# Experts 1 to 7 of a routed SwiGLU alternate the other way round: most tokens first, then fewest

## The chip, the cores and the metric

The kernel runs on one core of one Trainium2 chip. The metric is the device time of one execution in microseconds (us). The kernel before takes 1568.33 us, the median of three runs (1568.23 to 1573.31 us).

## What is computed

The reference is a two-layer streaming encoder on 256 tokens of width 1024, all in float32. Layer 0 has a pooling and state-space mixer and a dense feed-forward; layer 1 has a Mamba-2 mixer and then a routed feed-forward with eight experts, of which each token uses two. The change touches the order of the experts in that last part alone:

```python
def _moe_swiglu(h, w_router, b_router, w_gate, w_up, w_down):
    ...
    top_logit, top_idx = lax.top_k(logits, TOP_K)          # TOP_K = 2
    top_w = jax.nn.softmax(top_logit, axis=-1)
    ...
    for e in range(N_EXPERTS):                              # 8
        y_e = _swiglu(tok, w_gate[e], w_up[e], w_down[e])   # 1024 -> 3584 -> 1024
        out = out + gates[:, e:e + 1] * y_e
```

The sum over the experts can be taken in any order. Each expert has 3 x 1024 x 3584 float32 weights, 44.0 MB, and all eight are used.

## The kernel before

The routed part runs from about 714 us to the end. The weights of one expert come from HBM in 42 pieces of 1 MiB (`ITEM = 42`), in the fixed order `ORDER`: four steps t over the hidden columns, each with a gate product (`g`), an up product (`u`) and, one step later, the down product (`d`). Steps 0 to 2 have four pieces of each kind, step 3 has two of each. SyncE issues all these loads (line 462, in `load_expert`), expert after expert in one unbroken stream. They go round through 20 places in SBUF (`PIECES = 20`: 14 halves of `ring` and 6 areas of `arena`), so piece n may only be issued when TensorE has used piece n - 20; `first_pass_ready` waits for that on the semaphore `tile_used`. TensorE waits for each piece to land before it uses it (lines 1925 and 1961 are the matmuls of `hidden` and `output` in `expert`).

The experts are worked on in eight turns. Turn 0 is always expert 0, since its weights are loaded before the routing is known. The routing (lines 1225 to 1267) counts each expert's tokens. `make_turns` (lines 1284 to 1312, VectorE) then gives experts 1 to 7 their turns: `rank` is the number of experts with fewer tokens (0 to 6, ties broken by the number of the expert), and lines 1297 to 1300 turn the rank into a place from 1 to 7. A table of counts, flags and expert numbers by turn (`turn_i`) is released by `turns_ready`; SyncE takes the expert's number of each turn from it before it loads that expert's pieces, and TensorE, VectorE and ScalarE take the count, from which they choose one of three forms of the same program: (blocks, tokens a block) = (1, 64) up to 64 tokens, (3, 32) for 65 to 96, (2, 64) above. The form sets how long TensorE takes for a piece. The three forms use the same pieces in the same order.

Between two turns TensorE gathers the tokens of the next expert (`gather`, line 1417), scatters the outputs of the expert before the present one (`scatter`, line 1897) and turns hidden columns (line 1942). In the last turn the gather is replaced by the gate rows (line 1466). After the last turn come a last scatter, the norm and the store.

The lines of the rule before:

```python
c.inc(ts(place[:, 1:NE], rank, -2.0, 2.0 * n, ALU.mult, ALU.add), step)   # n = 7: 14 - 2 rank
c.then(ts(rank, rank, 2.0, 1.0, ALU.mult, ALU.add), step)                 # 2 rank + 1
...
c.then(tt(place[:, 1:NE], place[:, 1:NE], rank, ALU.min), step)
```

Of the kernel before, what the change touches and what calls it, by code (L numbers as in the profile page):

```python
# [13 lines left out]
ALU = mybir.AluOpType  # L14
# [19 lines left out]
NE = 8  # L34
# [92 lines left out]
def hybrid_trunk(nc, a, out):  # L127
    with ExitStack() as ctx:
# [774 lines left out]
        def _(dve):  # L903
            c = Counted(dve)
            v = nc.vector
            tt, ts, stt = v.tensor_tensor, v.tensor_scalar, v.scalar_tensor_tensor
            step = "dve_step"
# [192 lines left out]
            for t in range(6):  # L1100
                for j in range(2 if t == 5 else 4):
                    n = 4 * t + j
# [181 lines left out]
            def make_turns():  # L1284

                n = NE - 1
                own = totals[:, 1:NE].unsqueeze(2).broadcast_to([P, n, n])
                other = totals[:, 1:NE].unsqueeze(1).broadcast_to([P, n, n])
                less = order_tmp[:, 0:n * n].rearrange("p (e f) -> p e f", e=n)
                same = order_tmp[:, 64:64 + n * n].rearrange("p (e f) -> p e f", e=n)  # L1290
                rank, place = rt[:, 1, 0, 1:NE], rt[:, 1, 1]
                c.inc(tt(less, other, own, ALU.is_lt), step)
                c.then(tt(same, other, own, ALU.is_equal), step)
                c.then(tt(same, same, earlier[:, 1:NE, 1:NE], ALU.mult), step)
                c.then(tt(less, less, same, ALU.add), step)
                c.then(v.tensor_reduce(rank, less, AX.X, ALU.add), step)
                c.inc(ts(place[:, 1:NE], rank, -2.0, 2.0 * n, ALU.mult, ALU.add), step)
                c.then(ts(rank, rank, 2.0, 1.0, ALU.mult, ALU.add), step)
                c.inc(v.memset(place[:, 0:1], 0.0), step)
                c.then(tt(place[:, 1:NE], place[:, 1:NE], rank, ALU.min), step)  # L1300
                c.then(tt(perm, place.unsqueeze(1).broadcast_to([P, NE, NE]),
                          slot_iota[:, 0:NE].unsqueeze(2).broadcast_to([P, NE, NE]), ALU.is_equal), step)
                moved = order_tmp[:, 0:6 * NE * NE].rearrange("p (k c e) -> p k c e", k=NE, c=6)
                table = slots_of[:, 0].rearrange("p e b i -> p (b i) e").unsqueeze(1).broadcast_to([P, NE, 6, NE])
                c.then(tt(moved, table, perm.unsqueeze(2).broadcast_to([P, NE, 6, NE]), ALU.mult), step)
                c.then(v.tensor_reduce(slots_by_turn, moved, AX.X, ALU.add), step)
                rows_ = order_tmp[0:1, 0:3 * NE * NE].rearrange("p (j k e) -> p j k e", j=3, k=NE)
                for j, row in enumerate((cnt_f[:, 0:NE], cnt_f[:, 17:17 + NE], slot_iota[0:1, 0:NE])):
                    c.inc(tt(rows_[:, j], perm[0:1], row.unsqueeze(1).broadcast_to([1, NE, NE]), ALU.mult), step)
                dve.wait_ge(s[step], c.n[step])  # L1310
                c.then(v.tensor_reduce(turn_f.rearrange("p (j k) -> p j k", j=3), rows_, AX.X, ALU.add), step)
                c.inc(v.tensor_copy(turn_i[:, :], turn_f[:, :]), "turns_ready")
# [71 lines left out]
            take_tokens(0, MOE0)  # L1384
            take_gates(0, gates_of[0], 0)
            make_turns()
            dve.wait_ge(s["turns_ready"], 1)
            for e in range(NE):
# [689 lines left out]
```

How the kernel before makes its waits and increments, by code:

```python
            def then(self, ins, name):  # L332
                self.inc(ins, name)
                self.eng.wait_ge(s[name], self.n[name])
# [12 lines left out]
        def past(eng, name, n):  # L347
            eng.wait_ge(s[name], n + 1)
# [25 lines left out]
        def first_counts(eng, name):  # L375
            for primed in PRIMED[name]:
                eng.sem_inc(s[primed], 1)
            eng.wait_ge(s["cnt_ready"], 1)
# [25 lines left out]
        @block.sync  # L405
# [58 lines left out]
            def first_pass_ready(n):  # L464
                at = PLACES[n % PIECES]
                if n < PIECES and at < PIECES0 - 2:
                    sp.wait_ge(s["tile_used"], LAST_OF[at // 2] + 1)
                elif n < PIECES and at < PIECES0:
                    sp.wait_ge(s["y1_mm"], NB * NG)
                    sp.wait_ge(s["cb_mm"], NB * NG)
                elif n < PIECES and ARENA_PIECES[at - PIECES0] == 0:
                    sp.wait_ge(s["z_mm"], 8)
                elif n < PIECES and ARENA_PIECES[at - PIECES0] in (6144, 8192):
                    sp.wait_ge(s["y_turned"], 8)
                    sp.wait_ge(s["sq_done"], 16)
                elif n < PIECES:
                    sp.wait_ge(s["x_ready"], 6)
                else:
                    sp.wait_ge(s["tile_used"], MOE0 + n - PIECES + 1)
            for i, (kind, n, sl) in enumerate(TILES):
                src, k, w = sources[kind](n)
                if LAST_USER[i] is not None:
                    sp.wait_ge(s["tile_used"], LAST_USER[i] + 1)
                elif sl == 3:
                    sp.wait_ge(s["rows_turned"], 1)
```

## Time and profile before

| | |
|---|---|
| median of three runs | 1568.33 us (1568.23 to 1573.31) |
| profiled execution | 1568.54 us, its span 1566.7 us |
| TensorE busy | 1503.1 us (96%) |
| VectorE, ScalarE, GpSimd busy | 405.7, 216.2, 82.8 us |
| DMA queue of SyncE | 482.52 MB, 79.9% of 16 engines' span |
| HBM read | 486.97 MB |
| mean granted TensorE clock | 0.995 |

All times in the rows are microseconds from the start of the span. Read first the 40 slices of the span, which are 39.2 us each: the busy shares of the engines stand above the share of the DMA engines and the rate in GB/s. The routed part is slices 19 to 40. Then the same stretch is cut by turns, with the busy time of each engine, the clock, and the share and rate of DMA. A turn runs from the first matmul of its first gate product to that of the next turn. In the views of the chain and of the instructions, "x8" or "x16" behind lines 1925 and 1961 counts matmuls; in form (1, 64) one piece is 8 matmuls (16 in step 3), in form (2, 64) twice and in form (3, 32) six times as many.

### The profile page before, as it was taken

The page shows a single profiled execution, that of the slowest core. Times are in us where ns is not written, and L with a number is a line of the kernel's source. Part 1 is how long each engine was busy: PE and PEld are TensorE (multiplying, and loading weights), DVE is VectorE, ACT ScalarE, POOL GpSimd, SP SyncE. Part 2 cuts the span into 40 slices and gives each one's busy share as a digit, 9 for nine tenths or more (in the row PEclk, how much of TensorE's full clock was granted, in tenths as well). Part 3 has the DMA queues.
Part 4 walks back from the last instruction along what each step waited for, and adds up shares of the span by engine and source line. Part 5 has one row for each costly group of instructions (what it writes and reads, how often), then busy time and mean ns, then how long its engine had stood idle before and what let it go on. Part 6 is the DMA issues. An engine that isn't in the chain of part 4 may idle for free.

```text
span 1566.7 us, 24483 instructions
## 1 busy us (share of the span) xinstructions
PE 1503.1 (96%) x10627; PEld 866.2 (55%) x10628; DVE 405.7 (26%) x903; ACT 216.2 (14%) x423; POOL 82.8 (5%) x105
## 2 busy tenths in 40 slices
PE   7999999999999999999998899999999899998996
PEld 6645787776688755454442443443466733566433
DVE  6792443221255555223010100010100010200202
ACT  3332200000331154220000000000000010000001
POOL 5260000000000012000000000000000000000000
PEclk9999999999999999999999999999999999999999
DMA  9777676765545425657999999979999999999995
GB/s 335 236 266 268 221 269 221 262 215 197 206 162 214 138 92 202 244 231 273 407 411 410 407 412 408 410 282 400 412 410 407 408 412 408 409 412 403 411 399 217
DMA packets 160078, 489.88 MB, mean 313 GB/s; under 512 B 15888, under 2 KB 18896, under 8 KB 147664
## 3 DMA queue, kind: packets, MB, share of 16 engines
q1 hardware_dynamic: 153024, 482.52, 79.9%
q10 hardware_dynamic: 6928, 5.56, 1.3%
q8 instruction: 94, 1.54, 0.4%
q14 instruction: 32, 0.26, 0.0%
HBM read 486.97 MB, written 1.08 MB: 312 GB/s over the span
## 4 chain that ended last, share of the span: by engine, by line
PE 87%; DMA 7%; DVE 2%; issue 2%; SPq 1%; ACT 0%; POOL 0%; DVEq 0%
PE bank L1925 28%; PE bank L1417 22%; PE bank L1961 14%; PE bank L1653 5%; DMA ring<-in_moe_w_down 5%; PE bank L1768 4%; PE bank L1833 4%; PE bank L1897 2%; DMA ring<-in_mix_w_in 1%; PE bank L1942 1%; SPq L462 1%; PE bank L1442 1%; PE bank L1783 1%; PE bank L1431 1%; DMA ring<-in_ada_w 1%
## 5 line engine op out<-in xcount | busy, mean ns | idle before, releaser
L1925 PE MATMUL bank<-ring,arena 128*32 128x256 f32 (+3 forms) x3448 | 349.2, 422 | 12.1 <-issue 6.2
L1417 PE MATMUL bank<-arena,ring 128*128 128x256 f32 x1264 | 279.4, 380 | 1.3 <-ACT arena L734 1.0
L1925 PEld LDWEIGHTS bank<-ring,arena 128*32 128x32 f32 (+1 forms) x3448 | 159.1, 120 | 189.2 <-issue 136.8
L1417 PEld LDWEIGHTS bank<-arena,ring 128*128 128x128 f32 x1264 | 237.4, 190 | 33.5 <-ACT arena L734 1.5
L1961 PE MATMUL bank<-ring,arena 128*32 128x256 f32 (+1 forms) x1456 | 182.8, 467 | 5.5 <-DMA ring<-in_moe_w_down 5.5
L1334 DVE TENSOR_TENSOR arena<-arena,bank 128x512 f32<-128x512 f32 (+2 forms) x44 | 24.4, 577 | 608.5 <-PE bank L1925 608.5
L1925 PE MATMUL bank<-arena 128*32 128x256 f32 (+3 forms) x1416 | 156.2, 427 | 4.9 <-issue 2.5
L1961 PEld LDWEIGHTS bank<-ring,arena 128*32 128x32 f32 (+1 forms) x1456 | 72.4, 121 | 104.6 <-issue 75.7
L1925 PEld LDWEIGHTS bank<-arena 128*32 128x32 f32 (+1 forms) x1416 | 68.8, 121 | 83.3 <-issue 57.4
L874 ACT ACTIVATE arena<-bank 128x512 f32<-128x512 f32 (+2 forms) x44 | 21.1, 508 | 584.9 <-PE bank L1942 528.7
L1653 PE MATMUL bank<-ring,arena 128*128 128x512 f32 x176 | 76.9, 594 | 1.5 <-PE bank L1417 1.5
L1961 PE MATMUL bank<-arena 128*32 128x256 f32 (+1 forms) x672 | 72.6, 444 | 2.3 <-issue 1.2
L1768 PE MATMUL bank<-ring,arena 128*128 128x512 f32 x128 | 57.7, 593 | 3.0 <-DVE hd L1190 3.0
L1653 PEld LDWEIGHTS bank<-ring,arena 128*128 128x128 f32 x176 | 33.0, 190 | 42.6 <-issue 42.6
L1833 PE MATMUL bank<-ring,arena 128*128 128x512 f32 x128 | 55.1, 592 | 0.0
L931 DVE SCALAR_TENSOR_TENSOR arena<-ring,cT,arena 128x512 f32<-128x512 f32 x70 | 52.6, 751 | 2.1
L1961 PEld LDWEIGHTS bank<-arena 128*32 128x32 f32 (+1 forms) x672 | 32.5, 119 | 37.3 <-issue 28.7
L1111 DVE TENSOR_TENSOR arena<-arena,bank 128x256 f32<-128x256 f32 x22 | 9.3, 421 | 137.8 <-PE bank L1417 137.8
L1320 DVE TENSOR_SCALAR arena<-bank,gs,mod 128x128 f32<-128x128 f32 x64 | 21.9, 403 | 84.3 <-PE bank L1417 84.3
L1417 PE MATMUL bank<-ring,arena 128*128 128x512 f32 x96 | 42.1, 595 | 1.3 <-ACT arena L720 1.1
L583 POOL TENSOR_TENSOR arena<-arena,ring 128x512 f32<-128x512 f32 x31 | 39.4, 1291 | 53.1 <-DVE arena L1078 37.6
L1833 PEld LDWEIGHTS bank<-ring,arena 128*128 128x128 f32 x128 | 24.2, 190 | 30.1 <-issue 30.1
(305 smaller groups left out, 1092.9 us busy)
## 6 DMA issues: line engine op xcount, KB each, us to landing
ring<-in_moe_w_gate SPq DMA_DIRECT2D x85, 1024.0 KB, 19.4
ring<-in_moe_w_down SPq DMA_DIRECT2D x79, 1024.0 KB, 18.6
ring<-in_moe_w_up SPq DMA_DIRECT2D x73, 1024.0 KB, 18.7
ring<-in_ada_w SPq DMA_DIRECT2D x24, 2048.0 KB, 9.0
arena<-in_moe_w_up SPq DMA_DIRECT2D x39, 1024.0 KB, 18.7
arena<-in_moe_w_down SPq DMA_DIRECT2D x33, 1024.0 KB, 17.9
arena<-in_moe_w_gate SPq DMA_DIRECT2D x27, 1024.0 KB, 19.2
ring<-in_m_w_in SPq DMA_DIRECT2D x12, 2048.0 KB, 7.9
```

The costliest lines, as they stand in the source:

```text
L583: c.inc(g.tensor_tensor(qq[q % 4][:, k], zz[q % 2][:, k:k + 2], tables[:, 1 - k, q:q + 1, :].broadcast_to([P, 2, TOK]), ALU.mult), "q_ready")
L874: ins = f(sg[:, b, 0:w], ps[b][:, 0:w], ACT.Silu)
L931: c.then(stt(o, w[:, kc], cT[:, kc, 0:1], o, ALU.mult, ALU.add), "ada_summed" if kc == KC - 1 else step)
L1320: ins = ts(hcur3[:, kc], bank(kc // 4, 4, P)[:, kc % 4], gs[:, kc:kc + 1], mod[:, 1, 3, kc:kc + 1], ALU.mult, ALU.add)
L1334: ins = tt(sg[:, b, 0:w], sg[:, b, 0:w], ps[2 + b][:, 0:w], ALU.mult)
L1417: ins = mm(out_, l, r, start=i == 0, stop=i == len(pairs) - 1, **kw)
L1653: ins = mm(ps[i][:, :], act_f[:, t % 2, j, P * b:P * b + P], w[:, j, HALF * h:HALF * h + HALF], start=t == 0 and j == 0, stop=t == 5 and j ...
L1768: ins = mm(ps[6 + zi % 2][:, :], hT[:, kc, P * b:P * b + P], w[:, kc], start=kc == 0, stop=kc == KC - 1)
L1833: ins = mm(ps[4 + i][:, :], yT1[:, 4 * t + j, P * b:P * b + P], w[:, j, HALF * h:HALF * h + HALF], start=t == 0 and j == 0, stop=t == 3 an ...
L1897: mm(ps[banks[i]][:, :], gates[:, P * (i // 2):P * (i // 2) + P], y_sb[:, HALF * (i % 2):HALF * (i % 2) + HALF], start=True, stop=True).th ...
L1925: ins = mm(ps[base + b // per][m * h:m * h + m, w * (b % per):w * (b % per) + w], hcur3[:, kc, m * b:m * b + m], sl[:, kc - half * rows, w ...
L1961: ins = mm(ps[4 + b // per][m * h:m * h + m, w * (b % per):w * (b % per) + w], actT[:, t % 2, b // per, n * (b % per) + i, m * q:m * q + m ...
```

## The change

Two constants of `make_turns` differ. The place of an expert was min(14 - 2 rank, 2 rank + 1) and becomes min(13 - 2 rank, 2 rank + 2):

```diff
@@ -1294,8 +1294,8 @@
                 c.then(tt(same, same, earlier[:, 1:NE, 1:NE], ALU.mult), step)
                 c.then(tt(less, less, same, ALU.add), step)
                 c.then(v.tensor_reduce(rank, less, AX.X, ALU.add), step)
-                c.inc(ts(place[:, 1:NE], rank, -2.0, 2.0 * n, ALU.mult, ALU.add), step)
-                c.then(ts(rank, rank, 2.0, 1.0, ALU.mult, ALU.add), step)
+                c.inc(ts(place[:, 1:NE], rank, -2.0, 2.0 * n - 1.0, ALU.mult, ALU.add), step)
+                c.then(ts(rank, rank, 2.0, 2.0, ALU.mult, ALU.add), step)
                 c.inc(v.memset(place[:, 0:1], 0.0), step)
                 c.then(tt(place[:, 1:NE], place[:, 1:NE], rank, ALU.min), step)
```

| turn | 1 | 2 | 3 | 4 | 5 | 6 | 7 |
|---|---|---|---|---|---|---|---|
| rank before | 0 | 6 | 1 | 5 | 2 | 4 | 3 |
| rank after | 6 | 0 | 5 | 1 | 4 | 2 | 3 |

Nothing else is touched: the instructions, the pieces and their order within an expert are the same.

## Rows read from the trace of the kernel before

**Rows 1.** The page: the span in 40 equal slices.

```profile
PE   7999999999999999999998899999999899998996
...
DMA  9777676765545425657999999979999999999995
GB/s 335 236 266 268 221 269 221 262 215 197 206 162 214 138 92 202 244 231 273 407 411 410 407 412 408 410 282 400 412 410 407 408 412 408 409 412 403 411 399 217
```

**Rows 2.** Busy time by stretch: turns 0 to 7.

```profile
core 0: us, PE busy (x) PEld busy (x) DVE busy (x) ACT busy (x) POOL busy (x), PEclk, DMA share, GB/s
...
713.90:794.20 80.30, 79.16 (x416) 31.65 (x416) 11.83 (x39) 5.31 (x9) 0.00 (x0) 1.00 0.97 382
794.20:893.60 99.40, 87.11 (x424) 33.50 (x424) 7.27 (x18) 4.62 (x9) 0.00 (x0) 1.00 1.02 410
893.60:1050.90 157.30, 156.53 (x807) 63.95 (x806) 11.87 (x26) 8.10 (x17) 0.00 (x0) 1.00 0.98 386
1050.90:1133.70 82.80, 82.80 (x429) 34.49 (x430) 10.44 (x23) 5.21 (x10) 0.00 (x0) 1.00 0.99 390
1133.70:1260.30 126.60, 122.43 (x2274) 82.46 (x2275) 10.94 (x26) 6.61 (x17) 0.00 (x0) 0.99 1.02 408
1260.30:1343.00 82.70, 82.70 (x428) 33.07 (x432) 11.60 (x27) 6.27 (x14) 0.00 (x0) 1.00 1.02 410
1343.00:1468.80 125.80, 121.39 (x2273) 79.12 (x2273) 10.93 (x26) 6.61 (x17) 0.00 (x0) 1.00 1.02 408
1468.80:1552.50 83.70, 81.78 (x407) 30.71 (x406) 10.26 (x18) 7.35 (x16) 0.00 (x0) 1.00 0.93 372
```

**Rows 3.** The chain that ended last: starts of turns 1 and 2 (start, us, what).

```profile
794.70 10.54 PE bank L1925 x48
...
894.37 41.42 PE bank L1925 x192
```

**Rows 4.** Instructions of TensorE in turn 1, from one piece to the twentieth behind it.

```profile
828.65 1.94 PE L1961 MATMUL bank<-ring,arena 128*64 128x512 f32 x8 [0.29 <-DMA ring<-in_moe_w_down]
831.32 1.94 PE L1925 MATMUL bank<-ring,arena 128*64 128x512 f32 x8 [0.73 <-DMA ring<-in_moe_w_gate]
...
880.29 1.94 PE L1961 MATMUL bank<-ring,arena 128*64 128x512 f32 x8 [0.56 <-DMA ring<-in_moe_w_down]
```

**Rows 5.** Busy time by stretch: that stretch of turn 1 alone.

```profile
828.60:880.30 51.70, 40.14 (x201) 13.88 (x202) 1.11 (x2) 1.96 (x4) 0.00 (x0) 1.00 1.03 409
```

**Rows 6.** The chain: four pieces' matmuls in forms (1, 64), (2, 64) and (3, 32).

```profile
743.52 6.87 PE bank L1961 x32
...
950.84 13.73 PE bank L1961 x64
...
1176.36 10.36 PE bank L1961 x192
```

**Rows 7.** Loads that SyncE issues late in turn 2 (start, us in issuing).

```profile
1018.79 3.83 SPq L462 DMA_DIRECT2D arena<-in_moe_w_up  x2
...
1032.54 3.91 SPq L462 DMA_DIRECT2D ring<-in_moe_w_down  x2
1044.07 0.33 SPq L462 DMA_DIRECT2D arena<-in_moe_w_down  x1
```

**Rows 8.** What SyncE's loads waited for, 894 to 1060 us (us in total, times, longest).

```profile
SPq L462 <- PE bank L1925: 48.1, 23, 5.1
SPq L462 <- PE bank L1961: 42.4, 12, 7.5
```

**Rows 9.** Instructions of TensorE at the end of turn 7.

```profile
1537.44 1.94 PE L1961 MATMUL bank<-ring,arena 128*64 128x512 f32 x8 [0.35 <-DMA ring<-in_moe_w_down]
...
1544.80 1.94 PE L1961 MATMUL bank<-ring,arena 128*64 128x512 f32 x8 [0.54 <-DMA ring<-in_moe_w_down]
```

**Rows 10.** Busy time by stretch: the last ten full microseconds of loads.

```profile
1530.00:1540.00 10.00, 9.19 (x74) 5.08 (x70) 0.42 (x1) 0.87 (x2) 0.00 (x0) 1.00 1.02 416
```

**Rows 11.** Instructions of VectorE in `make_turns`.

```profile
716.28 0.17 DVE L1297 TENSOR_SCALAR rt<-rt 128x7 f32<-128x7 f32 x1
```

## The prediction

> **What bounds the kernel now.** I read the slices first [rows 1]. From slice 20 to slice 39 the DMA share is 9 tenths or more and the rate 399 to 412 GB/s in all but one (282 GB/s in slice 27); TensorE is nearly full too. So the routed part is a race between one stream of loads and TensorE, and only the view by turns tells who leads when. In it [rows 2] the number of TensorE instructions names the form: about 430 is (1, 64), 807 is (2, 64), 2274 is (3, 32). So before, turns 0, 1, 3, 5 and 7 are small, turn 2 is the one large expert, turns 4 and 6 are middle ones.
>
> How long does a piece take? Four pieces cost TensorE 6.87, 13.73 and 10.36 us [rows 6], that is 1.72, 3.43 and 2.59 us a piece. The stream has a pace of its own, to be read where TensorE has nothing left and waits for every landing: in turn 1 it starts a piece at 828.65 and the twentieth behind it at 880.29 [rows 4], so 51.64 / 20 = 2.58 us a piece, at 409 GB/s [rows 5] (1.049 MB / 409 GB/s = 2.56). Small experts eat faster than the stream brings, the large one slower, the middle ones about as fast. One expert at the stream's pace is 42 x 2.58 = 108.4 us; an undisturbed small turn is 82.8 us (turn 3), the large one 157.3 us [rows 2].
>
> Three places then matter. In turn 1 TensorE runs dry: the turn takes 99.4 us instead of 82.8, 16.6 us of waiting [rows 2]. In turn 2 the opposite happens: the 20 places fill up. SyncE's loads wait for lines 1925 and 1961 35 times between 894 and 1060 us [rows 8]; late in the turn they come one every 3.4 us, then one after a pause of 7.6 us [rows 7], and the rate over turn 2 is 386 GB/s and over turn 3 390 [rows 2]. Against 410 that is 157.3 x 24 / 410 + 82.8 x 20 / 410 = 9.2 + 4.0 = 13.2 us in which the stream stood still. Third, the end: TensorE is dry again, it waits for each piece from 1537.44 to 1544.80 [rows 9]. So the end is set by the last landing: the sum of all transfers plus the time in which the stream stood still. TensorE's 16.6 us of waiting in turn 1 are not on that path.
>
> **The change, part by part.** The two edited instructions keep their shape and cost (0.17 us for the first [rows 11]); they run once, beside TensorE's turn 0. No instruction, wait, byte or queue is added, so nothing stands behind a new wait. The same 336 loads are issued by SyncE in the same places; only which expert they belong to moves. What moves is the large expert, from turn 2 to turn 1, and with it the middle ones, from 4 and 6 to 3 and 5. Turns 2 to 6 of the new kernel are small, middle, small, middle, small: exactly the forms of turns 3 to 7 before.
>
> - *Turn 1.* The large turn starts at 794.7 instead of 894.4 [rows 3]. It never runs dry: it eats a piece in 3.43 us. It starts with more pieces landed than turn 2 did before: during the old turn 1 the stream moved 99.4 x 410 GB/s = 40.75 MB = 38.9 pieces and TensorE used 42, so the stock was 3.1 pieces smaller at the end of that turn than at its start. Hence the 20 places fill 3.1 pieces earlier and the stream stands still for 3.1 x 2.58 = 8.0 us more, 21 us in all.
> - *Turns 2 to 6.* Full places wipe out the history: at the end of the large turn all 20 are filled or being filled in either kernel. From there the new kernel repeats the old one from the end of its turn 2, 894.37 - 794.70 = 99.7 us earlier. The old one ended its turn 7 just dry [rows 9], so the new one ends turn 6 just dry, the transfers of turn 6 landing 99.7 us before the old last ones. Turn 6 has a gather where turn 7 had the gate rows; the stream runs on beside both, so that costs nothing.
> - *Turn 7.* One small expert is left, and TensorE has no stock for it: it goes at the stream's pace, 42 x 2.58 = 108.4 us. The tail behind the last pieces is the same as before.
>
> Sum: 1568.54 (the profiled execution, 0.2 us from the median) - 99.7 + 108.4 = 1577.2 us, +8.7. The other road, more standing still by 8.0 us, gives 1576.5. For the price of 42 pieces the rows allow 107.4 (42 x 2.56 by the rate in the dry stretch [rows 5]) to 110 (2.62 us a piece: 1.5% below the pace of the dry stretch, three times the gap between the 410 and 408 GB/s of small and middle turns [rows 2]): +7.7 to +10.3, so 1576.2 to 1578.8. I take 108.4, as it is read off landings that TensorE really waited for.
>
> Put in other words, the change removes 16.6 us of TensorE waiting from turn 1 and hands it back in turns 6 and 7, with interest: 108.4 - 82.8 = 25.6 us.
>
> One property of the dry turn could make it dearer. In the dry stretch TensorE stops for about 0.5 us ahead of nearly every piece [rows 4] and is busy 40.1 of 51.7 us, and the granted clock stays 1.00, 2.4 GHz [rows 5]. The Trainium skill, page "TensorE: Matmul & The Clock Gate", section "HAM oscillation — how this bites in real kernels", says that matmul bursts broken by waits for DMA can drop to half clock each time. In this trace, with 0.5 us stops, it does not happen; the same stops are what the new turn 7 has.
>
> **The rivals.**
>
> - *TensorE is the bound after all (faster).* The 16.6 us of waiting go and nothing comes back: 1568.5 - 16.6 = 1551.9 us. It decides if the stream has stock left at the end, at least the 25.6 us that a small turn eats. Against: the waits at the end of turn 7 before [rows 9], and there the stock was used up by one small turn behind a middle one; the new order has two small ones there.
> - *The stream makes part of it good (no change).* If the stream, behind longer standing still, ran at the best rate seen, 416 GB/s [rows 10], turn 7 would take 42 x 2.52 = 105.9 us: 1574.7; and if the places were never full for longer than before, nothing is lost: 1568.5. For: ten-microsecond stretches at 416 exist. Against: averages over whole turns stay at 408 to 410 and stock is plainly at its limit in turn 2 [rows 7, 8]. The Trainium skill, page "HBM Reference", section "Specifications (TRN2)", gives about 425 GB/s for a core that streams alone; by that, an estimate, the 42 pieces would take 103.6 us and the time would be 1572.4. No stretch of this case shows that rate.
> - *The clock falls in the dry last turn (slower still).* A small piece would then take 2 x 1.72 = 3.43 us and the turn 42 x 3.43 = 144 us: 1568.5 - 99.7 + 144 = 1613. Against: the clock of 1.00 in the dry stretch [rows 5].
> - *The order is not what it says.* If the counts did not rank as the diff assumes, the forms by turn would stay: 1568.5. Against: the forms of the old turns fit the rule [rows 2], and min(13 - 2 rank, 2 rank + 2) gives each of 1 to 7 once.
>
> **How the numbers follow.** A measurement of this kernel can tell about 0.5%, 7.8 us, from no change. The forecast has 0.72: its centre is above that bound (1576.4) but its lower end is not, so I give 0.58 of it to slower and 0.14 to the same. The stream making part good 0.16 (same), TensorE as the bound 0.05 (faster), the falling clock 0.05 (slower), the order not as stated 0.02 (same). That makes 0.05 faster, 0.32 same, 0.63 slower. The range takes the whole forecast, a margin of 2 us above it for a pause of the stream that the rows don't show, and most of the second rival: 1569.5 to 1581, about 0.84.
>
> **What would show it.** By turns, the new profile should have: turn 1 with some 807 TensorE instructions, 157 us long, with no waits for DMA, DMA at 380 GB/s or less over turns 1 and 2 together and SyncE issuing a load every 3.4 us from about 890 us on instead of 1000; turns 2 to 5 starting near 951, 1034, 1161 and 1244 us; turn 6 dry only in its last few pieces; turn 7 starting near 1455 us, about 106 us long, with waits of 0.5 us ahead of most pieces; the last landing near 1558 us; span 1575.4 us. The step "full places wipe out the history" is wrong if turn 3 starts off this grid; the sum is wrong if the stream has another long pause in turns 3 to 5, or if turn 7 has few waits.

## The result, and the profile after

The changed kernel takes 1586.37 us (median; 1584.83 to 1587.79), against 1568.28 us for the kernel before. The ratio is 1.0115, interval 1.0093 to 1.0137: 18.1 us slower, where I forecast 8.7 us and a time of at most 1581 us. The profiled execution took 1584.83 us, its span is 1583.1 us.

The page's slices, to be laid beside [rows 1] (a slice is now 39.6 us):

```profile
PE   8999999999999999999989999999899999998976
...
DMA  9777686656445516649999888999999999999995
GB/s 336 242 251 265 218 293 224 229 211 240 159 173 200 179 54 229 256 187 359 408 411 408 305 288 328 406 411 407 408 410 408 409 410 397 409 413 405 411 403 217
```

Before, one of slices 20 to 39 was below 390 GB/s. Now it is three in a row (305, 288, 328), and they come earlier. The same by turns, with the columns of [rows 2]:

```profile
713.00:794.97 81.97, 79.16 (x417) 31.72 (x417) 11.44 (x36) 5.90 (x10) 0.00 (x0) 1.00 0.99 387
794.97:958.78 163.81, 159.69 (x806) 61.36 (x806) 8.71 (x21) 7.52 (x16) 0.00 (x0) 0.97 0.92 344
958.78:1041.50 82.72, 82.72 (x426) 33.08 (x425) 10.45 (x23) 5.21 (x10) 0.00 (x0) 1.00 0.99 391
1041.50:1167.27 125.77, 121.45 (x2273) 78.29 (x2272) 10.95 (x26) 6.61 (x17) 0.00 (x0) 1.00 1.02 408
1167.27:1249.98 82.71, 82.71 (x425) 33.08 (x424) 11.61 (x27) 6.26 (x14) 0.00 (x0) 1.00 1.02 410
1249.98:1377.38 127.40, 122.68 (x2273) 78.66 (x2272) 10.94 (x26) 6.61 (x17) 0.00 (x0) 0.99 1.02 405
1377.38:1465.99 88.61, 84.33 (x426) 32.93 (x425) 11.60 (x27) 6.27 (x14) 0.00 (x0) 1.00 1.02 409
1465.99:1568.90 102.91, 87.09 (x407) 29.54 (x406) 8.41 (x13) 5.70 (x11) 0.00 (x0) 1.00 0.95 380
```

The forms stand where the diff puts them: 806 instructions in turn 1, 2273 in turns 3 and 5. Turns 2 to 5 are copies of the old turns 3 to 6 [rows 2], each within 1.6 us. Turns 6 and 7 together are 191.5 us, where the forecast had some 192. From 1487.5 us on, turn 7 waits for its pieces as turn 1 did before [rows 4]; the first line below is the last wait of turn 6, the last line the same place in turn 7:

```profile
1452.75 1.94 PE L1961 MATMUL bank<-ring,arena 128*64 128x512 f32 x8 [0.56 <-DMA ring<-in_moe_w_down]
...
1530.67 1.94 PE L1925 MATMUL bank<-ring,arena 128*64 128x512 f32 x8 [0.62 <-DMA ring<-in_moe_w_up]
...
1561.19 1.94 PE L1961 MATMUL bank<-ring,arena 128*64 128x512 f32 x8 [0.53 <-DMA ring<-in_moe_w_down]
```

The two are 42 pieces and 108.44 us apart, the price that the forecast put on the last turn.

What does not fit is turns 0 and 1: 82.0 + 163.8 = 245.8 us. The same two forms took 794.70 - 715.00 = 79.7 us (from the first matmul of turn 0) and 156.6 us before: 236.3. So 9.5 us were lost there, and the chain shows where (start, us, what):

```profile
788.58 3.58 PE bank L1961 x16
792.17 2.80 issue
794.97 1.50 PE bank L1925 x4
796.47 4.12 issue
800.59 43.10 PE bank L1925 x188
```

TensorE stops for 2.80 us between the turns, does four matmuls, and stops for 4.12 us more. "Issue" is time in which it waited for nothing that the profile shows. Nor was it slow to get going for lack of pieces: by the times of issue and some 18.5 us from issue to landing, about 7 of turn 1's had landed. The clock by stretch shows the rest of the loss:

```profile
792.20:794.90 2.70, 0.00 (x0) 0.00 (x0) 0.69 (x1) 0.59 (x1) 0.00 (x0) 1.00 1.02 399
794.90:796.50 1.60, 1.50 (x4) 0.23 (x4) 0.00 (x0) 0.00 (x0) 0.00 (x0) 0.69 1.03 410
796.50:800.60 4.10, 0.01 (x2) 0.01 (x2) 0.00 (x0) 0.00 (x0) 0.00 (x0) 0.50 1.03 407
800.60:805.00 4.40, 4.40 (x12) 1.32 (x14) 0.00 (x0) 0.00 (x0) 0.00 (x0) 0.50 1.03 410
805.00:810.00 5.00, 5.00 (x24) 1.55 (x22) 0.00 (x0) 0.00 (x0) 0.00 (x0) 0.93 1.03 409
```

The granted clock falls to 0.50 (1.2 GHz) during the pauses and stays there until after 805 us. The two pauses take 6.9 us where one of 0.53 us stood before turn 1; the other 3 us are matmuls at half clock.

What is special about this place? TensorE's program has a block of code for each expert and form. Behind each block stands a compare and branch (`to_expert`). Behind the (1, 64) block, the last of its expert, come the next expert's blocks in the order of `FORMS`: (3, 32), (2, 64), (1, 64). So after a small turn the (3, 32) block comes straight behind the branch. The branch to (1, 64) carries a hint, put out a turn earlier (`next_count`). The branch to (2, 64) jumps over the whole (3, 32) block and has none. The old kernel made that jump too, before its turn 2; it cost 0.77 us there. My theory now (A): the jump to a far block of code costs several microseconds, depending on where in the code it lands, and at this place TensorE's own time is what the kernel waits for. The rival (B): the pause is harmless, and the two small experts at the end cost more than I worked out.

### The profile page after: what moved, and what is told of

It is laid out like the page before. It is cut to its first block, busy times and chain, and to the rows that moved or that the text cites. A ratio compares the mean times of both kernels' runs of the same rounds, so it can differ in the third digit from the quotient of the medians.

```text
span 1583.1 us, 24483 instructions
## 1 busy us (share of the span) xinstructions
PE 1508.3 (95%) x10627; PEld 855.2 (54%) x10628; DVE 406.1 (26%) x903; ACT 216.1 (14%) x423; POOL 82.9 (5%) x105
## 3 DMA queue, kind: packets, MB, share of 16 engines
q1 hardware_dynamic: 153024, 482.52, 79.7%
## 4 chain that ended last, share of the span: by engine, by line
PE 87%; DMA 7%; DVE 2%; issue 2%; SPq 1%; ACT 0%; POOL 0%; DVEq 0%
PE bank L1925 29%; PE bank L1417 22%; PE bank L1961 14%; PE bank L1653 5%; PE bank L1768 3%; PE bank L1833 3%; DMA ring<-in_moe_w_down 3%; PE bank L1897 2%; DMA ring<-in_moe_w_gate 1%; DMA ring<-in_mix_w_in 1%; PE bank L1942 1%; SPq L462 1%; PE bank L1442 1%; PE bank L1783 1%; PE bank L1431 1%
## 5 line engine op out<-in xcount | busy, mean ns | idle before, releaser
L1925 PE MATMUL bank<-ring,arena 128*32 128x256 f32 (+3 forms) x3456 | 358.3, 425 | 17.0 <-issue 9.4
L1925 PEld LDWEIGHTS bank<-ring,arena 128*32 128x32 f32 (+1 forms) x3456 | 157.3, 120 | 206.0 <-issue 146.0
L1925 PE MATMUL bank<-arena 128*32 128x256 f32 (+3 forms) x1408 | 149.9, 419 | 7.6 <-issue 2.8
L1961 PEld LDWEIGHTS bank<-ring,arena 128*32 128x32 f32 (+1 forms) x1432 | 69.5, 122 | 112.5 <-issue 79.5
L1925 PEld LDWEIGHTS bank<-arena 128*32 128x32 f32 (+1 forms) x1408 | 64.7, 120 | 84.4 <-issue 58.0
L1961 PE MATMUL bank<-arena 128*32 128x256 f32 (+1 forms) x696 | 76.9, 446 | 1.2 <-DMA arena<-in_moe_w_down 1.2
L1961 PEld LDWEIGHTS bank<-arena 128*32 128x32 f32 (+1 forms) x696 | 31.8, 118 | 40.2 <-issue 28.8
## 6 DMA issues: line engine op xcount, KB each, us to landing
ring<-in_moe_w_up SPq DMA_DIRECT2D x73, 1024.0 KB, 18.5
arena<-in_moe_w_gate SPq DMA_DIRECT2D x27, 1024.0 KB, 20.3
```

The costliest lines, as they stand in the source:

```text
L1925: ins = mm(ps[base + b // per][m * h:m * h + m, w * (b % per):w * (b % per) + w], hcur3[:, kc, m * b:m * b + m], sl[:, kc - half * rows, w ...
L1961: ins = mm(ps[4 + b // per][m * h:m * h + m, w * (b % per):w * (b % per) + w], actT[:, t % 2, b // per, n * (b % per) + i, m * q:m * q + m ...
```

## The experiments

In each case "from turn 0 to the last matmul" is the sum of the eight turns in the run's own trace, 837.5 us before and 855.9 after; it leaves out what differs ahead of the routed part, where turn 0 began between 713.0 and 719.7 us.

**The code of the large form laid nearest.** For both orders:

```diff
-            FORMS = ((3, 32), (2, 64), (1, 64))
+            FORMS = ((2, 64), (3, 32), (1, 64))
```

> The changed kernel, with the code of the large form (2, 64) laid directly behind each branch, in the place of the form (3, 32). Theory A (a code jump cost 9.5 us of the 18.1): the pauses of 2.8 and 4.1 us of TensorE at the start of turn 1 and the half clock behind them are gone, turn 1 takes 157 us instead of 166, and the time is near the forecast of 1577 us (+8 to +10 against the kernel before). Pauses at the start of turns 3 and 5 (now the far form) may appear, but the stream is not standing still there, so they cost nothing. Theory B (the two small experts at the end cost more than I thought, the pause is harmless): the time stays at 1586 us.

Measured: 1577.99 us, ratio 1.0052 (1.0031 to 1.0072). Turns 0 to 3 and 6 to 7:

```profile
716.23:795.22 78.99, 78.99 (x417) 31.78 (x419) 10.76 (x35) 5.31 (x9) 0.00 (x0) 1.00 0.98 387
795.22:951.68 156.46, 156.46 (x809) 61.17 (x805) 9.38 (x22) 8.10 (x17) 0.00 (x0) 1.00 0.96 367
951.68:1035.23 83.55, 82.78 (x426) 33.13 (x426) 11.10 (x24) 5.79 (x11) 0.00 (x0) 1.00 0.99 391
1035.23:1169.26 134.03, 125.11 (x2271) 78.74 (x2271) 10.28 (x26) 6.02 (x16) 0.00 (x0) 0.96 1.02 409
...
1380.56:1463.28 82.72, 82.72 (x425) 34.43 (x425) 10.10 (x24) 4.75 (x10) 0.00 (x0) 1.00 1.02 408
1463.28:1561.90 98.62, 85.93 (x407) 29.93 (x406) 8.40 (x13) 5.70 (x11) 0.00 (x0) 1.00 0.95 382
```

Turn 1 is 156.5 us, busy without a gap, at full clock. The pause has moved with the far form to turn 3: 134.0 us instead of 125.8, clock 0.96. There it costs nothing: the stream runs at 409 GB/s through that turn, and turn 7 still waits for its pieces (busy 85.93 of 98.62 us). The same jump ahead of turn 5 costs 0.90 us. The whole is 8.5 us above the kernel before (1569.49 in the same comparison); A holds, B falls.

> The kernel before with the same new layout of the code, as a control. Theory A: 1568 us, no change: turn 2 began with a pause of only 0.8 us, and turns 4 and 6, where the far form now is, run with the stream never standing still. If the layout itself is worth something, this one moves too, and the pair has to be compared with each other.

Measured: 1577.33 us, ratio 1.0052 (1.0035 to 1.0068). I had expected no change, so this is a miss, and the most useful one. Turns 2, 6 and 7, then the instructions at the start of turn 6:

```profile
892.10:1048.62 156.52, 156.52 (x808) 61.24 (x807) 11.88 (x26) 8.10 (x17) 0.00 (x0) 1.00 0.98 388
...
1344.52:1479.53 135.01, 125.71 (x2272) 81.55 (x2272) 10.16 (x25) 6.02 (x16) 0.00 (x0) 0.96 1.02 408
1479.53:1560.46 80.93, 80.93 (x407) 31.05 (x406) 10.25 (x18) 7.34 (x16) 0.00 (x0) 1.00 0.81 321
```

```profile
1344.52 1.07 PE L1925 MATMUL bank<-ring,arena 128*32 128x256 f32 x16 [0.92 <-issue]
1350.27 4.07 PE L1925 MATMUL bank<-ring,arena 128*32 128x256 f32 x36 [4.68 <-issue]
```

The far form is now the middle one, and the jump before turn 6 costs 0.92 + 4.68 us and half clock: 135.0 us instead of 125.8. I had argued that this is free because the stream never stands still there. But only one small turn is left behind it. It needs 25.6 us of stock to run without a wait, and the old turn 7 began with nearly all of that: it took 83.7 us [rows 2, 9]. More stock than that is worth nothing. In turn 7 TensorE now never waits (80.93 of 80.93 us busy): the end is TensorE's. From turn 0 to the last matmul it is 847.2 us, 9.7 more. The same pause that was free in turn 3 of the other order costs in full in turn 6 of this one.

**One part of the change at a time**, both with the near layout. Four small VectorE instructions behind the minimum exchange places 1 and 2:

```diff
                 c.then(tt(place[:, 1:NE], place[:, 1:NE], rank, ALU.min), step)
+                c.then(ts(rank, place[:, 1:NE], -2.0, 3.0, ALU.mult, ALU.add), step)
+                c.then(ts(less[:, 0, 0:n], place[:, 1:NE], 2.5, None, ALU.is_lt), step)
+                c.then(tt(rank, rank, less[:, 0, 0:n], ALU.mult), step)
+                c.then(tt(place[:, 1:NE], place[:, 1:NE], rank, ALU.add), step)
```

> From the kernel before with the new layout: turns 1 and 2 alone exchange their experts (ranks 6, 0, 1, 5, 2, 4, 3). The theory of the full places: the whole price lies in turn 1, where the large expert meets a larger stock, so this costs the same +8 to +10 as the changed order: 1577 us. The rival, that the pair of small experts at the end sets the price: here the end is as before (middle, small), so the time would be 1568.

Measured: 1579.88 us, ratio 1.0064 (1.0044 to 1.0083). The stream stands still in turn 1 as in the full change (367 GB/s, also there):

```profile
793.41:949.87 156.46, 156.46 (x808) 61.12 (x805) 9.39 (x22) 8.10 (x17) 0.00 (x0) 1.00 0.96 367
```

By the rates, turns 1 and 2 hold 156.5 x 43 / 410 + 82.7 x 20 / 410 = 20.4 us of standing still, 7.2 more than the 13.2 of the kernel before; I had worked out 8.0. So the exchange of turns 1 and 2 alone makes the stream stand still as long as the full change does. The time does not show what that costs: the order unswapped in this layout takes 1577.33 us, for the other reason, and here too TensorE never waits in turn 7 (80.94 of 80.95 us busy). It is the rate of turn 1 (367 against 410) that carries the verdict.

> From the kernel before with the new layout: turns 1 and 2 as before, the pairs 3, 4 and 5, 6 exchanged (ranks 0, 6, 5, 1, 4, 2, 3). The theory of the full places: behind the large expert the 20 places are full, and now a middle expert follows, in whose 126.6 us the stream could bring 49 pieces while 42 are used; so it stands still for 6 to 7 pieces more, 16 to 18 us: 1585 us, although this is half of the change and leaves turn 1 alone. The rival, that only the place of the large expert counts: 1568.

Measured: 1582.98 us, ratio 1.0091 (1.0065 to 1.0116), from turn 0 to the last matmul 852.0 us. Turns 2 to 4:

```profile
893.08:1050.09 157.01, 156.59 (x808) 61.21 (x808) 12.18 (x27) 8.43 (x18) 0.00 (x0) 1.00 0.98 388
1050.09:1175.60 125.51, 121.38 (x2272) 78.19 (x2272) 11.31 (x27) 6.87 (x18) 0.00 (x0) 1.00 0.92 352
1175.60:1259.22 83.62, 82.78 (x425) 33.11 (x425) 12.30 (x29) 6.86 (x15) 0.00 (x0) 1.00 0.99 391
```

A middle turn behind the large one runs at 352 GB/s: 125.5 x 58 / 410 = 17.8 us in which the stream stands still. In the old turn 4, the same form, it was 408 [rows 2]. This half of the change, which leaves the large expert in its turn, costs 14.5 us alone (852.0 against 837.5; 13.5 by the medians), and here turn 7 does wait for its pieces (85.26 of 96.55 us busy), so it is the landings that the time shows. In the full change the two don't add up, because a small turn follows the large one there again. Full places as the mechanism are shown by this; the rival is out.

**Five microseconds of TensorE in turn 0.** In both orders, 24 dummy matmuls:

```diff
                 turn_hidden(3)
                 after_turns()
+                if first_pass and k == 0:
+                    stay_warm(24, 2)
```

> The changed order with the near layout, and 24 dummy matmuls (some 5 us of TensorE) in turn 0 behind the last turning of the hidden columns. Theory: until the end of the large turn no landing is waited for and the places fill up, so TensorE's own time counts in full there: +5 us against the same kernel without them, 1583 us, and the last landing moves by the same 5 us. Rival: TensorE's lost time is made good somewhere, then 1578.

Measured: 1581.26 us, ratio 1.0089 (1.0065 to 1.0114), 3.3 above the kernel without them (each against the kernel before in its own comparison: 12.6 and 8.5 us, 4.1 apart); from turn 0 to the last matmul 850.9 us against 845.7, so +5.2, the whole length of the dummies.

> The same 24 dummy matmuls in turn 0 of the order of before, near layout. Theory: turn 1 waits for landings for some 16 us there, so the 5 us vanish in that wait: 1577 us as without them, with turn 1 shorter by 5 us. Rival: 5 us of TensorE cost 5 us wherever they stand: 1582.

Measured: 1581.97 us, ratio 1.0084 (1.0067 to 1.0100), 4.6 above its partner. By time, the rival; by the trace (847.5 us against 847.2) the theory. The two profiled executions took 1578.62 and 1576.45 us, and 1.9 of those 2.2 us had arisen ahead of turn 0. I took it as open and ran it again, on the kernel's own layout, where the end is a landing, and once more with the near layout.

> The kernel before in its own layout of the code, with the 24 dummy matmuls (5 us of TensorE) in turn 0. The pair with the near layout left it open: by its traces turn 1 took the 5 us in, by its times 4 us were lost, but there the end is TensorE's and hangs on the pauses of turns 4 and 6. Here the end is the last landing. Theory: turn 1 gets 5 us shorter, the last landing does not move, 1568.5 to 1570 us. Rival: 1573.5 us.

Measured: 1568.16 us, ratio 0.9999 (0.9989 to 1.0009). Turns 0 to 2:

```profile
713.16:797.51 84.35, 84.35 (x465) 37.20 (x467) 10.75 (x35) 5.31 (x9) 0.00 (x0) 1.00 0.99 389
797.51:892.35 94.84, 85.89 (x427) 32.39 (x423) 7.91 (x19) 5.20 (x10) 0.00 (x0) 1.00 1.02 410
892.35:1048.87 156.52, 156.52 (x807) 63.92 (x807) 11.24 (x26) 7.51 (x16) 0.00 (x0) 1.00 0.98 386
```

Turn 0 is 4.7 us longer than before, turn 1 is 4.8 shorter, and nothing is lost. So 5 us of TensorE in turn 0 cost nothing where a dry turn follows and cost 5 us where the large one follows. That is why the pauses ahead of the large turn counted in full there.

> The order of before with the near layout once more, beside the next one on the same chip, with more rounds: 1577 us; last turn held by TensorE.

> The near layout with the 24 dummy matmuls once more. Theory: what it loses beside the run before this one are the pauses of turns 4 and 6, where its code lies 48 instructions or more further on, and not turn 0: turn 2 starts at the same distance from turn 0, and a difference in time shows as longer turns 4 to 6. If turn 2 starts 5 us later, the theory of the dry turn is wrong.

Measured: 1579.17 and 1580.93 us (ratios 1.0057, 1.0037 to 1.0078, and 1.0074, 1.0059 to 1.0088). Turns 0 and 1 together are 178.8 and 179.3 us: turn 2 does not start 5 us later. Turns 5 and 6 take 89.4 and 128.8 us with the dummies, where it was 83.8 and 134.5 without: the pause before turn 6 is now one of 6.6 us and falls ahead of the turn's first matmul. From turn 0 to the last matmul they differ by 1.2 us, and 1.7 us of the 2.9 between the two profiled executions had arisen ahead of turn 0. (The code lies 96 instructions further on and not 48: the trace has 48 more matmuls and as many more weight loads in turn 0.) That this explains all of the 4.6 us of the first pair is not shown; the two intervals overlap this time.

**Where the code lies.** Two kernels keep the changed order and the old `FORMS` and shift only the code. The first puts 16 dummy matmuls at the very start of TensorE's program (`stay_warm(WARM_ROWS + 16, 5)`).

> The changed kernel with its own layout of the code and 16 more dummy matmuls at the very start of TensorE's program, which do nothing but move all code behind them by 64 instructions. Theory: the first pause at the start of turn 1 (2.8 us, the jump over the code of another form) stays, and the second one, 4.1 us behind four matmuls, is gone, since four matmuls in was the end of a fetched block of code; with it goes most of the half clock. Turn 1 starts up to 7 us less late, the time is 1579 to 1582 us. Rival: both pauses are a matter of the form and stay: 1586.

Measured: 1583.46 us, ratio 1.0089 (1.0072 to 1.0105). TensorE at the start of turn 1, and turns 0 and 1:

```profile
796.50 2.31 PE L1961 MATMUL bank<-ring,arena 128*64 128x512 f32 x10
801.60 4.92 PE L1925 MATMUL bank<-ring,arena 128*64 128x512 f32 x14 [2.79 <-issue]
```

```profile
719.65:801.60 81.95, 79.16 (x416) 31.68 (x417) 11.44 (x36) 5.90 (x10) 0.00 (x0) 1.00 0.98 388
801.60:959.81 158.21, 158.21 (x806) 64.36 (x807) 8.70 (x21) 7.51 (x16) 0.00 (x0) 0.99 0.94 355
```

The first pause stays within a hundredth, the second is gone, turn 1 falls from 163.8 to 158.2 us, and from turn 0 to the last matmul it is 849.2 us, 6.7 less. So 64 instructions at the far end of the program, in a stretch that does no work, take away a 4 us pause in turn 1. Beside the place of the code only the moment changed: turn 0 began 6.6 us later. That this moves such pauses is unlikely by the two profiles of the order of before with the near layout: turn 0 began at 713.22 and 716.18 us, and the pauses of turn 6 were 0.92 + 4.68 and 0.97 + 4.48 us. The later start also takes back what turn 1 won: the profiled executions of this kernel and of the changed one both took 1584.83 us, while the medians differ by 2.9.

The second puts 16 dummy matmuls behind the last down product of turn 0 (`stay_warm(16, 2)` behind `output(3)`), where turns 1 to 6 have a scatter.

> The changed kernel with 16 dummy matmuls (3.4 us, as long as a scatter) behind the last down product of turn 0. They move the code behind them by 64 instructions, as the kernel with the padding did. Theory: turn 0 is the only turn that ends without a scatter, so nothing runs while the code of the large form is fetched; with the dummies the fetch runs beside them, the first pause is below 1 us instead of 2.8, the second one is absent, and turn 0 with pause is 82.4 to 83.4 us. Turn 1 takes 156.5 us at the full clock. Time 1579 to 1580. Rival: the fetch begins only when TensorE has finished; then the pause stays at 2.8 us behind the dummies, turn 0 takes 85 us, and the time is 1582.

Measured: 1585.44 us, ratio 1.0099 (1.0082 to 1.0117). A miss for theory and rival: there is one pause, of neither expected length, and the clock falls to 0.50 again.

```profile
794.13 3.84 PE L1424 MATMUL bank<-ident 128*128 128x128 f32 x32
802.14 9.49 PE L1925 MATMUL bank<-ring,arena 128*64 128x512 f32 x32 [4.17 <-issue]
```

So matmuls in front of the jump don't hide it here, though the code behind them lies where it lay in the kernel with the padding.

What TensorE waits for in these pauses can be read from the traces. The view of DMA has a queue called "instruction" with packets of 16 KiB (94 of them, 1.54 MB, in the kernel before). Read in stretches of 0.1 us, it shows one such packet at each pause (us from the start of the span):

| kernel and place | TensorE stopped | packet | TensorE went on | pause |
|---|---|---|---|---|
| before, ahead of turn 1 | 794.17 | 791.9 | 794.70 | 0.53 |
| before, ahead of turn 2 | 893.60 | 891.7 | 894.37 | 0.77 |
| changed, ahead of turn 1 | 792.17 | 792.3 | 794.97 | 2.80 |
| changed, inside turn 1 | 796.47 | 798.1 | 800.59 | 4.12 |
| 16 dummies at the start, ahead of turn 1 | 798.81 | 798.9 | 801.60 | 2.79 |
| 16 dummies behind turn 0, ahead of turn 1 | 797.97 | 799.4 | 802.14 | 4.17 |
| before, turn 4, step 3 | 1225.85 | 1224.8 | 1227.47 | 1.62 |
| before, turn 4, step 3 | 1231.17 | 1231.1 | 1233.72 | 2.55 |

In each row TensorE goes on 2.5 to 2.8 us after the packet. So the pauses are waits for code, and their length is set by when the packet comes: 1.9 us before TensorE was done in the old turn 2, and only when it was done, or later, in the changed kernel. The kernel with the near layout has such a packet at 793.4 and no pause (turn 1 starts at 795.22). What sets the moment of the packet stays open.

**Two places fewer** (`PIECES` 18 instead of 20), in the order of before.

> The kernel before with 18 places for pieces instead of 20. Theory of the full places: the large expert fills them two pieces earlier, so the stream stands still for 2 x 2.58 = 5.2 us more, once: 1573.5 us. The rival, that standing still is set by something else (the pauses between turns, SyncE), gives no change.

Measured: 1576.53 us, ratio 1.0050 (1.0033 to 1.0066): 7.9 us where I expected 5.2. Turns 0 to 2:

```profile
713.25:793.02 79.77, 79.15 (x416) 31.67 (x417) 11.31 (x36) 5.87 (x10) 0.00 (x0) 1.00 0.98 387
793.02:897.50 104.48, 88.69 (x424) 32.99 (x425) 7.35 (x19) 4.63 (x10) 0.00 (x0) 1.00 1.02 410
897.50:1054.18 156.68, 156.59 (x807) 63.95 (x807) 11.22 (x26) 7.51 (x16) 0.00 (x0) 1.00 0.96 373
```

I had overlooked that the places are full twice: already ahead of turn 0, while the router is worked out (SyncE issues no load between 696 and 717 us before, and none between 695 and 715 us with 18 places). Two pieces fewer lie ready there, and the dry turn 1 is 4.8 us longer; then the large turn fills the smaller store sooner (373 GB/s instead of 386, 5 us). Each place is worth some 2.4 us at each time that all are full. From turn 0 to the last matmul it is 8.5 us more; two places twice at 2.58 us each would be 10.3, so the rule of one piece's time for each place is right in kind and 1.8 us too high.

## Why the prediction was wrong, point by point

- *What bounds the kernel, and where the stream stands still*: right. Adding 5 us to TensorE in the two orders, taking away two places, and the two half exchanges came out on the side that it names, the exchange of turns 1 and 2 by its rates and not by its time.
- *Full places wipe out the history*: right. Turns 2 to 5 repeat the old turns 3 to 6. The sign that I had named for it would have said the opposite: turn 3 started at 1041.5 us and not near 1034. But that offset was there when turn 2 began, at 958.8 where 951 was forecast.
- *Turn 7 at the stream's pace, 108.4 us where 99.7 are saved*: right. The last waits of turns 6 and 7 are 108.4 us apart. Turns 2 to 7 of the changed kernel are 610.1 us (the six rows above), and the old turn 1 (99.7) and turns 3 to 7 (501.5) are 601.2 [rows 2, 3]: +8.9 us, forecast +8.7. With the pauses gone, the changed order measured +8.5.
- *"The large turn starts at 794.7 instead of 894.4"*, and runs as it did: this step failed. I took over the old turn's 157 us, with a gap of 0.77 us ahead of it, wrote that no instruction and no wait was added, and so priced the switch to the large form at nothing. Turns 0 and 1 lost 9.5 us to two pauses of TensorE, in which it waited for code, and to half clock behind them. 8.9 + 9.5 = 18.4 us, the difference from turn 0 to the last matmul; the median moved by 18.1.
- *Standing still of 21 us*: right only without the pauses. The near layout has 156.5 x 43 / 410 + 83.6 x 19 / 410 = 20.3 us in turns 1 and 2; the changed kernel as it is has 163.8 x 66 / 410 + 82.7 x 19 / 410 = 30.2. TensorE's lost 9.5 us fill the places that much earlier.
- The rival *TensorE is the bound*, with its point at 25.6 us of stock, did not happen in the changed kernel; it did in the old order with the near layout, from a pause in turn 6. The rival *the clock falls in the dry last turn* is out: turn 7 shows 1.00. The clock fell elsewhere, in the pauses. *The stream makes part good* is out: 42 pieces took 108.4 us, the old pace. *The order is not what it says* is out by the forms of the turns.

The trace of before held the clue: the gap of 0.77 us ahead of the large turn, larger than the one ahead of turn 1, and "issue" gaps inside turns 4 and 6, none of them explained by a wait. Those inside the turns stand where no branch is, in step 3 of the form (3, 32), with 128 matmuls (and as many weight loads) from one to the next:

```profile
1227.47 3.70 PE L1925 MATMUL bank<-ring,arena 128*32 128x128 f32 x128 [1.62 <-issue]
1233.72 2.56 PE L1925 MATMUL bank<-ring,arena 128*32 128x128 f32 x41 [2.55 <-issue]
```

They come in the middle turns of either order, so they do not enter the difference, but with their packets (last two rows of the table above) they show that TensorE can stop for its code without a jump too. The Trainium skill, page "Runtime: NRT & Kernel Launch", section "Instruction fetch mechanics", says that code is refilled in 16 KiB blocks, in sequence, and that a taken branch to a block not at hand makes the engine wait for a fetch. It speaks against this change, and I had not weighed it. The runs agree: shifting code by 64 instructions takes one pause of 4.1 us away, laying the block next to the branch takes both, and a packet of 16 KiB stands at each pause. What a jump costs had to come from the runs.

No kernel here beats the one before; its far jump costs little where it stands, and it has a small turn ahead of the large one to empty the places.

## What to carry to other kernels

With a stream of loads through a ring of buffers that sets the end, the time is all transfers plus the time in which the ring is full, so order the work such that the slowest user starts on an empty ring and a fast one follows it. An engine's lost microsecond is free while it is ahead of the loads and costs in full between the last dry point and the moment the ring is full; ask of every new cost on which side it falls. A change of order also changes which block of code follows which: price the jump, too, at the place where it lands.

## What was new about the hardware

- A jump over a large block of TensorE's code cost 0.8 to 7 us, by where the code lies: 2.8 + 4.1 us, 2.8 alone after a shift of 64 instructions, 4.2 in a third layout, 5.1 and 0.9 us at two places of one kernel (turns 3 and 5 of the changed order, near layout), none when the block stands next to the branch.
- TensorE went on 2.5 to 2.8 us after a packet of the instruction queue, in all eight pauses of the table, with a jump and without one; the pause is as long as that packet is late.
- Two pauses of 2.8 and 4.1 us with four matmuls between them brought the granted clock to 0.50 until after 805 us, 3 us more on top. Behind a single pause of 2.79 us it was 0.58 and 0.65 in the next 4.4 us. Stops of about 0.5 us ahead of nearly every piece, for 74 us in turn 7, left it at 1.00.
